# Raw expert blocks under the first tile's staging buffer, gathered rows under the others'

## The chip, the cores and the metric

The kernel runs on 1 core of one Trainium2 chip. The metric is the device time of one execution in microseconds (us), as the median of several runs. The core has a matrix engine (PE, with its weight loads as PEld), a vector engine (DVE), a scalar engine (ACT), a general one (POOL) and a queue engine that only issues transfers (SP). Sixteen DMA engines move what SP and POOL issue.

## What is computed

One decoder layer on 512 tokens of 1024 channels. The change lies in its second half, where every token picks, for each of 8 heads, the 16 best of 16,384 experts, each a pair of rows u and v:

```python
def peer_ffn(h, w_query, sub_keys, expert_u, expert_v):
    ...
    e = (jnp.take_along_axis(i1, flat // PEER_TOPK, axis=-1) * PEER_NKEYS
         + jnp.take_along_axis(i2, flat % PEER_TOPK, axis=-1))
    g = jax.nn.softmax(sc, axis=-1).astype(h.dtype)
    def one_chunk(args):
        xc, ec, gc = args
        u = expert_u[ec]
        a = jax.nn.gelu(jnp.einsum('cd,chkd->chk', xc, u))
        return jnp.einsum('chk,chkd->cd', gc * a, expert_v[ec])
```

## The kernel before, in words

The kernel splits the tokens of this part. Some 320 of them (two tiles of 128 and half of a third, `DS`) are computed densely: all 128 blocks of 128 experts are loaded in full, and a token's gate for an expert that it didn't pick is zero. The other 192 (192 = the fourth tile and half of the third, moved beside it) are computed by gathering the rows that they picked.

The dense part needs a table of gates, [expert, block, token]. It is built before the blocks ("the gate stage"): for each token DVE, POOL and ACT write one-hot rows, PE multiplies them (L853), and ACT copies the result out of PSUM into a staging buffer (`stage`, L1106), 4 tokens a group, 80 groups (`w_staged` counts them): 32 into `staged[0]`, 32 into `staged[1]`, 16 into `staged[2]`. SP stores each staging buffer to DRAM, to `w_scratch`: tile 0 and tile 1 whole (8 MB each, pieces of 512 B), tile 2 in slices of blocks, `SLICES` (pieces of 256 B, 32 KB a block). Later each block reads its own row of it back (`load_gates`, into `w_row`).

Memory is reused by address, in KB of a partition: `staged[0]` lies at 35.5 to 99.5, `staged[1]` at 99.5 to 163.5, `staged[2]` at 67.5 to 99.5, over the upper half of `staged[0]`. In the kernel before the raw blocks (`u_raw` and `v_raw`, 99.5 to 131.5) lie under `staged[1]`, and the gathered rows (`u_rows`, `v_rows`, 35.5 to 83.5) under `staged[0]` and `staged[2]`. The row of gates (`w_row`), and the parts of a block split in two for precision (`u_hi`, `u_lo`, `v_hi`, `v_lo`), lie under `staged[1]` in both.

Block b of the dense part, in the order in which each engine runs it (all run in order, and semaphores join them): ACT copies `u_raw` to `u_hi` (`u_high`, L1167), DVE makes `u_lo` (`u_low`, L1555), PE multiplies 24 times (`first`, L887 to L889), ACT takes the gelu (L1182), DVE multiplies with the gates (`gated`, L1568), ACT and DVE split that in two (`g_both`, L1188 and L1572), and PE multiplies with `v_hi` and `v_lo` 16 times (`second`, L900 to L910). On PE the order is first(b+1), second(b). On DVE, `block_step(b)` is gated(b), u_low(b+2), g_lo(b); then comes `own(n, q)`, a quarter of the gathered tokens' work (b = 4n + q): q = 0 and 1 use three gathered u rows each (L1587), q = 2 and 3 three v rows each (L1615); then `next_values`, which is v_low(b+1). On ACT, `block_step(b)` is gelu(b), u_high(b+2), g_hi(b), v_high(b+1).

The raw buffers hold 4 blocks (`STEP`). SP refills a place when its block has been used (`refill(n, q)`): u, v and gate row of block b+4. POOL gathers 6 u rows and 6 v rows of 512 KB for each 4 blocks (`gather_u`, `gather_v`, then `next_rows`).

SP's order in the handover, before: store tile 0, store tile 1, store slice 0 of tile 2; wait for tile 1's store; load blocks 0 to 3; wait for slice 0; load four gate rows; store slice 1; refill(0, 0); store slice 2; refill(0, 1) to refill(0, 3); wait for slices 1 and 2; the loop. POOL, behind its last one-hot rows, waits for `w_stored[0]`, gathers u rows, waits for slices 0 and 1, gathers v rows.

Of the kernel before, what the change touches and what calls it, by code (L numbers as in the profile page):

```python
# [13 lines left out]
P = 128  # L14
D = 1024
S = 512
NT = S // P
KD = D // P
# [6 lines left out]
PH, NK, QD = 8, 128, 128  # L25
# [22 lines left out]
ROWS = GRP + XGRP  # L48
DT = NT - 1
EX = P // 2  # L50
DS = DT * P - EX
STEP = 4
# [6 lines left out]
EARLY = 32  # L59
OWN, SPLIT = NT - 1, NT - 2  # L60
POOL_ROWS = 2
SLICES = [(0, 8), (8, 64), (64, NK)]


def bucket_onehot():
# [81 lines left out]
def build(nc, x, c, ada_w, ada_b, rows_g, w_in, ln_gb, w_s, b_s, rel, w_branch, w_out, w_query, keys,  # L147
# [3 lines left out]
    with ctx:  # L151
# [3 lines left out]
        def sem(name):  # L155
            return ctx.enter_context(nc.semaphore(name))
# [5 lines left out]
        def at(name, kb, shape, dt=F32):  # L162
            t = nc.alloc_sbuf_tensor_at(name, shape, dt, offset=base_byte + int(kb * 1024))
            return t[tuple(slice(None) for _ in shape)]
# [86 lines left out]
        staged = [at("staged0", 35.5, [P, NK, P]), at("staged1", 99.5, [P, NK, P]), at("staged2", 67.5, [P, NK, EX])]  # L251


        u_raw = at("u_raw", 99.5, [P, STEP, KD, P])
        v_raw = at("v_raw", 115.5, [P, STEP, D])
        w_row = at("w_row", 131.5, [P, STEP, DS])
        u_hi = at("u_hi", 137.5, [P, 2, KD, P], F32R)
        u_lo = at("u_lo", 145.5, [P, 2, KD, P], F32R)
# [2 lines left out]
        gel = at("gel", 169.5, [P, 2, DS])  # L261
        gated = at("gated", 172.5, [P, 2, DS])
        g_both = at("g_both", 177, [P, 2, DS, 2], F32R)
        u_rows = at("u_rows", 35.5, [P, ROWS, D])
        v_rows = at("v_rows", 59.5, [P, ROWS, D])
        acc_x = at("acc_x", 24, [P, D])
        fold = at("fold", 83.5, [P, 2, EX])
        y_out = at("y_out", 99.5, [P, DT, D])
        y_parts = at("y_parts", 111.5, [P, D])
        junk3 = at("junk3", 115.5, [P, D])  # L270
# [90 lines left out]
        w_stored = [sem(f"w_stored{i}") for i in range(2)]  # L361
        w_slice = [sem(f"w_slice{i}") for i in range(len(SLICES))]
        u_raw_in, v_raw_in, w_row_in = ([sem(f"{n}{q}") for q in range(STEP)]
# [20 lines left out]
        def turn(j, q):  # L384

            return j // STEP + 1
# [39 lines left out]
        def _(sp):  # L426
# [56 lines left out]
            def load_experts(q, b):  # L483

                sp.dma_start(u_raw[:, q].rearrange("p k e -> p (k e)"), u_blocks[b]).then_inc(u_raw_in[q], 16)
                sp.dma_start(v_raw[:, q], v_blocks[b]).then_inc(v_raw_in[q], 16)

            def load_gates(q, b):
                sp.dma_start(w_row[:, q], w_rows[b]).then_inc(w_row_in[q], 16)

            def store_gates(t, lo, hi, signal):

                sp.wait_ge(w_staged, min(DS_GROUPS * (t + 1), ALL_GROUPS))
                n = min(P, DS - t * P)
                sp.dma_start(w_dram[:, lo:hi, t * P:t * P + n], staged[t][:, lo:hi, 0:n]).then_inc(signal, 16)
# [6 lines left out]
            for half in range(2):  # L502
                rows, cut = slice(half * EX, (half + 1) * EX), slice(half * EX, (half + 1) * EX)
                sp.dma_start(ex_picks[rows, 0], starts[EX:P, cut]).then_inc(ex_in, 16)
                sp.dma_start(ex_picks[rows, 1], picks[SPLIT][EX:P, 2, cut]).then_inc(ex_in, 16)
            store_gates(0, 0, NK, w_stored[0])
            store_gates(1, 0, NK, w_stored[1])
            store_gates(2, *SLICES[0], w_slice[0])
            sp.wait_ge(w_stored[1], 16)
            for q in range(STEP):  # L510
                load_experts(q, q)
            sp.wait_ge(w_stored[0], 16)
            sp.wait_ge(w_slice[0], 16)
            for q in range(STEP):
                load_gates(q, q)

            def refill(n, q):
                b = n * STEP + q
                sp.wait_ge(u_lo_done, b + 1)
                sp.wait_ge(v_lo_done, b + 1)  # L520
                sp.wait_ge(gated_done, b + 1)
                load_experts(q, b + STEP)
                load_gates(q, b + STEP)

            for q in range(STEP):
                if q + 1 < len(SLICES):
                    store_gates(2, *SLICES[q + 1], w_slice[q + 1])
                refill(0, q)
            for q in range(1, len(SLICES)):
                sp.wait_ge(w_slice[q], 16)  # L530
# [13 lines left out]
        def _(pool):  # L544
# [96 lines left out]
            multiplied(pool, *group("h2T"))  # L641
            pool.wait_ge(idx_ready, 1)

            pool.wait_ge(w_stored[0], 16)
            for part in range(2):
                gather_u(0, part)
            pool.wait_ge(w_slice[0], 16)
# [28 lines left out]
        def _(pe):  # L676
# [45 lines left out]
            def project(*jobs):  # L722
                for _, b, j in jobs:
                    w = arrived("in", b)
                    cut = slice(j * P, (j + 1) * P)
                    product(("in", b, j), [(w[:, k, cut], hT[:, k, :]) if b < 2 else (hT[:, k, cut], w[:, k, :])
                                           for k in range(KD)])
# [213 lines left out]
        def _(act):  # L941
# [42 lines left out]
            def gates(jobs):  # L984

                for _, b, j in jobs:
                    o = take(act, "in", b, j)
                    gate, f = (ga, b - 5) if b < 7 else (gg, b - 7)
                    act.activation(gate[:, j, f * HALF:(f + 1) * HALF], o[:, :], ACT.Tanh, scale=0.5)\
                        .then_inc(free("in", b, j), 1)  # L990
# [171 lines left out]
            def u_high(j, q):  # L1162
                r = q % 2
                act.wait_ge(u_raw_in[q], 16 * turn(j, q))
                if not isinstance(j, int) or j >= 2:
                    act.wait_ge(a_full, j - 1)
                act.activation(u_hi[:, r], u_raw[:, q], ACT.Copy).then_inc(u_hi_done, 1)  # L1167
# [24 lines left out]
            def own_gelu(n):  # L1192

                act.wait_ge(u_rows_used[1], n + 1)
                act.activation(dots_gelu, dots, ACT.Gelu_apprx_tanh).then_inc(own_gelu_done, 1)

            u_high(0, 0)
            u_high(1, 1)
            v_high(0, 0)
# [32 lines left out]
        def _(dve):  # L1232
# [342 lines left out]
            def next_values(b, q):  # L1575
                if not isinstance(b, int) or b + 1 < NK:
                    v_low(b + 1, (q + 1) % STEP)
# [47 lines left out]
            for q in range(STEP):  # L1625
                block_step(q, q)
                own(0, q)
                next_values(q, q)
            dve.wait_ge(w_slice[len(SLICES) - 1], 16)
            two = ident.rearrange("p (t a) -> p t a", a=2)  # L1630
# [58 lines left out]
```

## Time and profile before

| | us |
|---|---|
| median of 3 runs | 1782.34 (1781.99 to 1784.86) |
| the profiled execution's own time | 1783.35 |
| its span in the profile | 1781.6 |
| PE busy | 1600.2 (90%) |
| DVE busy | 1306.5 (73%) |
| POOL busy | 828.0 (46%) |
| ACT busy | 600.4 (34%) |

The span is cut by the profile into 40 slices of 44.5 us. A digit in them is a share in tenths. The gate stage ends at 791 us, in the eighteenth slice; the 128 blocks fill the rest. All stretches below are in us from the start of the span.

### The profile page before, as it was taken

To read this page: it belongs to the slowest core of one execution; us is meant where nothing else is said; L and a number is where in the kernel's file an instruction comes from. 1 tells how busy PE (TensorE), PEld (TensorE's weight loads), DVE (VectorE), ACT (ScalarE), POOL (GpSimd) and SP (SyncE) were. 2 spreads that over 40 slices of the span, in tenths; PEclk is the share of its full clock that TensorE was granted. 3 is DMA by queue.
4 is the path that set the end of the run, shared out by engine and by line. 5 is a ranking of instruction groups with operands and counts; after the bars stand their busy time and mean duration, and the time that the engine had idled before them with its cause. 6 is when DMAs were issued, how large, how long until landed. Compare 5 with 4: busy or idle time off the path is not lost.

```text
span 1781.6 us, 24636 instructions
## 1 busy us (share of the span) xinstructions
PE 1600.2 (90%) x7621; PEld 1241.8 (70%) x7621; DVE 1306.5 (73%) x2599; ACT 600.4 (34%) x1043; POOL 828.0 (46%) x800
## 2 busy tenths in 40 slices
PE   6899999999797764666699999999999999999997
PEld 2444454444475653556599999999999999999996
DVE  0534231213259999974699999999999999999998
ACT  1120022320213665332233433343343344334333
POOL 1000100000103996672566666666666666666662
PEclk9899999999898985898799999999999999999998
DMA  9946211111300000679999999999999999999993
GB/s 360 341 154 224 94 60 47 48 47 66 126 1 1 1 1 13 190 208 337 370 388 388 378 387 380 385 388 385 383 384 384 381 385 385 386 384 384 384 383 120
DMA packets 192870, 450.39 MB, mean 253 GB/s; under 512 B 30323, under 2 KB 79731, under 8 KB 192444
## 3 DMA queue, kind: packets, MB, share of 16 engines
q1 hardware_dynamic: 136636, 245.21, 38.7%
q0 software_dynamic: 56192, 204.66, 29.3%
q8 instruction: 21, 0.34, 0.1%
q14 instruction: 21, 0.17, 0.0%
HBM read 426.13 MB, written 23.10 MB: 252 GB/s over the span
## 4 chain that ended last, share of the span: by engine, by line
PE 78%; DVE 11%; DMA 6%; POOL 2%; issue 1%; ACT 1%; SPq 1%; POOLq 0%; DVEq 0%; ACTq 0%
PE bank L693 22%; PE bank L888 8%; PE bank L889 8%; PE bank L887 8%; PE bank L910 7%; PE bank L908 6%; PE bank L909 6%; PE bank L900 3%; PE bank L901 3%; DMA w_scratch<-staged 2%; PE bank L814 2%; DMA u_raw<-u_by_key 2%; DMA ada_blk<-ada_w 2%; POOL hot L625 1%; PE bank L778 1%
## 5 line engine op out<-in xcount | busy, mean ns | idle before, releaser
L887 PE MATMUL bank<-h_hi,u_hi 128*128 128x320 f32 x1024 | 316.6, 309 | 22.9 <-DVE u_lo L1555 22.9
L888 PE MATMUL bank<-h_lo,u_hi 128*128 128x320 f32 x1024 | 317.4, 310 | 0.0
L889 PE MATMUL bank<-h_hi,u_lo 128*128 128x320 f32 x1024 | 317.3, 310 | 0.0
L601 POOL DMA_INDIRECT v_rows<-v_exp,small x192 | 263.1, 1370 | 91.5 <-POOL small L597 51.8
L601 POOL DMA_INDIRECT u_rows<-u_exp,small x192 | 240.9, 1255 | 92.5 <-POOL small L597 52.0
L1174 ACT ACTIVATE v_hi<-v_raw 128x1024 fp32r<-128x1024 f32 x128 | 135.8, 1061 | 245.6 <-PE bank L910 245.6
L1555 DVE TENSOR_TENSOR u_lo<-u_raw,u_hi 128x1024 fp32r<-128x1024 f32 x128 | 157.6, 1231 | 75.3 <-ACT u_hi L1167 75.3
L887 PEld LDWEIGHTS bank<-h_hi,u_hi 128*128 128x128 f32 x1024 | 193.1, 189 | 28.3 <-issue 23.1
L910 PE MATMUL bank<-v_hi,g_both 128*128 128x512 f32 x512 | 204.4, 399 | 0.0
L909 PE MATMUL bank<-v_lo,g_both 128*128 128x512 f32 x512 | 203.2, 397 | 0.0
L908 PE MATMUL bank<-v_hi,g_both 128*128 128x512 f32 x512 | 203.2, 397 | 0.0
L693 PE MATMUL bank<-ring,hT 128*128 128x512 f32 x448 | 197.8, 598 | 0.8 <-ACT zv L1004 0.8
L888 PEld LDWEIGHTS bank<-h_lo,u_hi 128*128 128x128 f32 x1024 | 193.0, 188 | 6.8
L889 PEld LDWEIGHTS bank<-h_hi,u_lo 128*128 128x128 f32 x1024 | 193.0, 188 | 0.0
L597 POOL COPY small<-idx_by 128x3 uint32 (+1 forms) x128 | 119.2, 931 | 148.0 <-DVE acc L1615 81.4
L1615 DVE SCALAR_TENSOR_TENSOR acc<-v_rows,small,acc 128x1024 f32<-128x1024 f32 x128 | 164.1, 1282 | 8.6 <-DMA v_rows<-v_exp,small 6.4
L693 PEld LDWEIGHTS bank<-ring,hT 128*128 128x128 f32 x448 | 84.7, 191 | 109.1 <-issue 109.1
L1561 DVE TENSOR_TENSOR v_lo<-v_raw,v_hi 128x1024 fp32r<-128x1024 f32 x128 | 155.9, 1218 | 0.0
L1587 DVE SCALAR_TENSOR_TENSOR u_rows<-u_rows,h_own 128x1024 f32<-128x1024 f32 x128 | 153.5, 1218 | 0.0
L1167 ACT ACTIVATE u_hi<-u_raw 128x1024 fp32r<-128x1024 f32 x128 | 134.7, 1052 | 44.7 <-DMA u_raw<-u_by_key 44.7
L1182 ACT ACTIVATE gel<-bank 128x320 f32<-128x320 f32 x128 | 56.0, 438 | 242.4 <-PE bank L889 242.4
L900 PE MATMUL bank<-v_hi,g_both 128*128 128x512 f32 x256 | 101.9, 398 | 19.0 <-DVE g_both L1572 19.0
(216 smaller groups left out, 2589.7 us busy)
## 6 DMA issues: line engine op xcount, KB each, us to landing
u_raw<-u_by_key SPq DMA_DIRECT2D x128, 512.0 KB, 6.1
v_raw<-v_exp SPq DMA_DIRECT2D x128, 512.0 KB, 8.1
w_row<-w_scratch SPq DMA_DIRECT2D x128, 160.0 KB, 9.3
ada_blk<-ada_w SPq DMA_DIRECT2D x9, 2048.0 KB, 17.7
ring<-w_in SPq DMA_DIRECT2D x9, 2048.0 KB, 8.4
w_scratch<-staged SPq DMA_DIRECT2D x2, 8192.0 KB, 34.6
ring<-ada_w SPq DMA_DIRECT2D x3, 2048.0 KB, 13.0
xr<-x SPq DMA_DIRECT2D x8, 512.0 KB, 11.7
```

What stands on the lines that cost most here:

```text
L601: pool.indirect_dma_start(out=rows[:, s], out_offset=None, in_=table, in_offset=bass.IndirectOffsetOnAxis(ap=ix[:, s:s + 1], axis=0))\
L693: last = pe.matmul(o[:, :], a, b, start=(k == 0), stop=(k == len(pairs) - 1))
L887: pe.matmul(o, u_hi[:, r, k], h2_hi[:, k], start=(k == 0), stop=False)
L888: pe.matmul(o, u_hi[:, r, k], h2_lo[:, k], start=False, stop=False)
L889: last = pe.matmul(o, u_lo[:, r, k], h2_hi[:, k], start=False, stop=(k == KD - 1))
L900: pe.matmul(o, both, v_hi[:, r, half], start=is_first, stop=False)
L908: pe.matmul(o, hi, v_hi[:, r, half], start=is_first, stop=False)
L909: pe.matmul(o, hi, v_lo[:, r, half], start=False, stop=False)
L910: last = pe.matmul(o, lo, v_hi[:, r, half], start=False, stop=is_last)
L1555: dve.tensor_tensor(u_lo[:, r], u_raw[:, q], u_hi[:, r].bitcast(F32), ALU.subtract)\
L1561: dve.tensor_tensor(v_lo[:, r], v_raw[:, q], v_hi[:, r].bitcast(F32), ALU.subtract)\
L1615: ins = dve.scalar_tensor_tensor(into, v_rows[:, s], coef[:, s:s + 1], into, ALU.mult, ALU.add)
```

## The change

The raw blocks move under `staged[0]`, to the lower half that `staged[2]` doesn't cover. The gathered u rows move under `staged[1]`, the v rows and `fold` under `staged[2]`. Tile 2 is stored in two slices instead of three: blocks 0 to 7, and 8 to 127. SP waits for tile 0's store as soon as it has issued it, loads blocks 0 to 3, and only then comes to tile 1's store. The whole second slice is issued behind the four gate rows and ahead of all refills. POOL's first u gather waits for tile 1's store instead of tile 0's, and ACT waits for tile 1's store before it writes `u_hi`. POOL's first v gather still waits for slices 0 and 1, but slice 1 is now all that is left of the tile.

```diff
-SLICES = [(0, 8), (8, 64), (64, NK)]
+SLICES = [(0, 8), (8, NK)]
...
-        u_raw = at("u_raw", 99.5, [P, STEP, KD, P])
-        v_raw = at("v_raw", 115.5, [P, STEP, D])
+        u_raw = at("u_raw", 35.5, [P, STEP, KD, P])
+        v_raw = at("v_raw", 51.5, [P, STEP, D])
...
-        u_rows = at("u_rows", 35.5, [P, ROWS, D])
-        v_rows = at("v_rows", 59.5, [P, ROWS, D])
+        u_rows = at("u_rows", 99.5, [P, ROWS, D])
+        v_rows = at("v_rows", 67.5, [P, ROWS, D])
...
-        fold = at("fold", 83.5, [P, 2, EX])
+        fold = at("fold", 91.5, [P, 2, EX])
...
             store_gates(0, 0, NK, w_stored[0])
+            sp.wait_ge(w_stored[0], 16)
+            for q in range(STEP):
+                load_experts(q, q)
             store_gates(1, 0, NK, w_stored[1])
             store_gates(2, *SLICES[0], w_slice[0])
             sp.wait_ge(w_stored[1], 16)
-            for q in range(STEP):
-                load_experts(q, q)
-            sp.wait_ge(w_stored[0], 16)
             sp.wait_ge(w_slice[0], 16)
             for q in range(STEP):
                 load_gates(q, q)
+            store_gates(2, *SLICES[1], w_slice[1])
...
             for q in range(STEP):
-                if q + 1 < len(SLICES):
-                    store_gates(2, *SLICES[q + 1], w_slice[q + 1])
                 refill(0, q)
...
-            pool.wait_ge(w_stored[0], 16)
+            pool.wait_ge(w_stored[1], 16)
             for part in range(2):
                 gather_u(0, part)
...
+            act.wait_ge(w_stored[1], 16)
             u_high(0, 0)
```

## Rows read from the trace of the kernel before

**Rows 1.** The span in 40 equal slices: PE's busy tenths.
```profile
PE   6899999999797764666699999999999999999997
```
**Rows 2.** Stretches: length, each engine's busy us (instructions), granted clock, DMA share, GB/s.
```profile
720.00:750.60 30.60, 22.81 (x150) 20.31 (x151) 30.30 (x91) 10.75 (x18) 22.41 (x30) 0.83 0.97 275
750.60:769.70 19.10, 15.94 (x112) 13.33 (x112) 19.10 (x56) 8.37 (x14) 15.86 (x22) 1.00 0.00 0
769.70:791.80 22.10, 17.96 (x126) 14.97 (x125) 19.81 (x58) 9.56 (x16) 17.95 (x24) 1.00 0.96 274
791.80:808.20 16.40, 0.00 (x0) 0.00 (x0) 0.00 (x0) 0.00 (x0) 5.09 (x7) 0.60 1.04 345
...
830.00:839.00 9.00, 9.00 (x54) 8.36 (x54) 7.76 (x13) 3.93 (x7) 6.72 (x6) 1.00 1.08 295
839.00:861.00 22.00, 7.70 (x44) 6.79 (x42) 5.21 (x5) 0.44 (x1) 11.99 (x15) 0.74 1.06 403
...
900.00:1000.00 100.00, 100.00 (x555) 91.30 (x555) 93.75 (x124) 40.47 (x60) 68.57 (x56) 1.00 1.01 384
```
**Rows 3.** The chain that ended last, 769 to 862: start, length, what.
```profile
769.68 38.51 DMA w_scratch<-staged
...
812.31 10.13 DMA w_row<-w_scratch
...
829.86 31.71 DMA u_raw<-u_by_key
```
**Rows 4.** SP's instructions in order of time: start, length of the issue.
```profile
814.56 0.42 SPq L495 DMA_DIRECT2D w_scratch<-staged  x1
...
829.86 20.52 SPq L485 DMA_DIRECT2D u_raw<-u_by_key  x1
```
**Rows 5.** DMA issues at 720, 814, 829, and all u gathers: size, us to landing.
```profile
w_scratch<-staged SPq DMA_DIRECT2D x1, 8192.0 KB, 30.7
...
w_scratch<-staged SPq DMA_DIRECT2D x1, 1792.0 KB, 15.3
...
w_scratch<-staged SPq DMA_DIRECT2D x1, 2048.0 KB, 29.7
...
u_rows<-u_exp,small POOLq DMA_INDIRECT x192, 8.1
```
**Rows 6.** PE's instructions in order of time, with the idle time before them.
```profile
813.95 0.61 PE L887 MATMUL bank<-h_hi,u_hi 128*128 128x320 f32 x1 [22.90 <-DVE u_lo L1555]
...
824.71 0.47 PE L900 MATMUL bank<-v_hi,g_both 128*128 128x512 f32 x1 [1.28 <-DVE g_both L1572]
...
864.46 0.76 PE L900 MATMUL bank<-v_hi,g_both 128*128 128x512 f32 x1 [17.77 <-DVE g_both L1572]
...
874.34 0.39 PE L900 MATMUL bank<-v_hi,g_both 128*128 128x512 f32 x1
...
881.59 0.39 PE L900 MATMUL bank<-v_hi,g_both 128*128 128x512 f32 x1
```
**Rows 7.** ACT, POOL and DVE in order of time, each with its idle time before.
```profile
811.49 1.06 ACT L1167 ACTIVATE u_hi<-u_raw 128x1024 fp32r<-128x1024 f32 x1 [19.72 <-DMA u_raw<-u_by_key]
...
789.71 0.18 POOL L597 COPY small<-idx_by 128x3 uint32<-128x3 uint32 x1
...
793.52 0.94 POOL L601 DMA_INDIRECT u_rows<-u_exp,small  x1 [0.30 <-issue]
...
830.04 0.69 POOL L597 COPY small<-idx_by 128x3 uint32<-128x3 uint32 x1 [31.11 <-DMA w_scratch<-staged]
...
844.14 1.28 DVE L1615 SCALAR_TENSOR_TENSOR acc<-v_rows,small,acc 128x1024 f32<-128x1024 f32 x1 [6.37 <-DMA v_rows<-v_exp,small]
...
848.87 0.49 DVE L1568 TENSOR_TENSOR gated<-gel,w_row 128x320 f32<-128x320 f32 x1
```
**Rows 8.** Stretches with PE idle, and its restart: columns as in rows 2.
```profile
849.00:851.00 2.00, 0.00 (x0) 0.00 (x0) 0.35 (x1) 0.00 (x0) 1.70 (x2) 0.64 1.04 407
...
864.00:867.00 3.00, 2.54 (x6) 2.09 (x7) 2.96 (x4) 1.35 (x2) 0.00 (x0) 0.50 1.04 403
```

## The prediction

> **What bounds the kernel now.** I read the slices first [rows 1]. PE is at 9 tenths in every slice from the twenty-first on (from 888 us): once the blocks run, PE sets the pace, and this stretch can't get shorter by moving transfers. The hundred microseconds from 900 to 1000 [rows 2] say the same: PE busy 100.00 of 100, at full clock, with DMA at 384 GB/s. The `second` of block 4 starts on PE at 874.34 and that of block 5 at 881.59 [rows 6]: a block costs 7.25 us. Everything behind 874.34 I take as fixed, since the code there is the same. So the question is when the second(4) starts in the changed kernel. I call that time S4; before it is 874.34.
>
> Next the stretch in front of it, by windows [rows 2]. In the gate stage, to 791, PE is held by hot rows; DMA moves 275 GB/s to 750.6 (tile 0's store), nothing at all to 769.7, then 274 GB/s (tile 1's store). From 791.8 to 808.2 every compute engine but POOL stands still. The chain [rows 3] names it: tile 1's store, from 769.68 for 38.51 us; behind it a gate row that takes 10.13 us; and then a u block from 829.86 for 31.71 us. PE has two holes [rows 6]: 22.90 us before 813.95 and 17.77 us before 864.46, the second(3). A handover in which PE never waited after its second(0) at 824.71 would have S4 at 824.71 + 4 x 7.25 = 853.7; it is 20.6 later. These two holes are what the change can touch.
>
> **Tile 1's store.** Before, POOL gathers six u rows (3.15 MB) beside it: it takes their indices at 789.71 and issues the third at 793.52 [rows 7]; from 791.8 to 808.2 DMA is fully busy, at 345 GB/s [rows 2]. The change holds these gathers back until the store has landed. Tile 0's store, of the same size and with nothing beside it, took 30.7 us [rows 5]. So tile 1's should land at 769.7 + 30.7 = 800.4 instead of 808.2 (769.68 + 38.51): 7.8 us earlier. I call this T1.
>
> **The first loads.** SP gets an added wait, for tile 0's store, at about 750.7. Queued behind it are eight loads and tile 1's store, which isn't ready before 769.7. The eight issues took from 808.2 to 812.3 [rows 3], 4.1 us, and the 4.19 MB take 10.4 us at 403 GB/s [rows 2]: done by about 765, in a window in which DMA is empty. The gate stage shouldn't notice: PE does 112 instructions in 19.1 us with DMA idle (5.9 a microsecond) and 126 in 21.3 us of work with DMA full (5.9) [rows 2]. Cost zero; without that cover (if the loads ran past 769.7) they would delay T1 by what is left. ACT then starts `u_hi` right at T1. Before it waited until 811.49 [rows 7], 3.3 us behind the store, and PE began 2.46 us after ACT [rows 6, 7]. So first(0) starts at about 800.5 + 2.5 = 803.0 instead of 813.95.
>
> **The gate rows and second(0).** Slice 0 (256 KB) follows tile 1's store in the queue, 1 us by 274 GB/s, so the gate rows are issued at 801.4 with no loads in front of them; before, the first took 10.13 us [rows 3] behind 4 MB. The second(0) then hangs on PE alone, two `first`s behind 803.0: about 812.5 instead of 824.71. That is 12.2 us gained at this point, before the next steps.
>
> **POOL's first u gather.** Moved from 789.7 to T1. Queued behind its wait on POOL are only the v gathers. By the old pace the third row is issued 3.8 us after the wake [rows 7] and takes 8.1 [rows 5]: 812.5, just when own(0, 0) wants it. If it is some microseconds late this doesn't count, because DVE has to wait for v rows further on, at 840, and would reach that point at about 827.
>
> **The merged slice.** This is what sets the end. The first v gather needs all of tile 2 stored. Before, slice 1 landed at 829.86 (814.56 + 15.3 [rows 4, 5]); now it is blocks 8 to 127, 120 x 32 KB = 3.93 MB, issued at 801.4 + 2.25 (four gate issues, 812.31 to 814.56 [rows 3, 4]) = 803.7. I call its landing T2. Between T1 + 1 = 801.4 and T2 the DMA engines have to move the gate rows (0.66 MB), the u gathers (3.15 MB) and this slice, 7.74 MB. Refills queue behind the slice. The rate has two bounds: 403 GB/s, where 256 B pieces, gathers and loads mix (839 to 861), gives 19.2 us, T2 = 821, and with a late start 822; 295 GB/s (830 to 839) [rows 2] gives 26.2, T2 = 827.6. A third way: old slice 1 could only move once the gate rows in front of it were in (822.44), so its 1.835 MB took 7.4 us, 247 GB/s; 3.93 MB at that rate is 15.9 us, and the other 3.81 MB at 403 is 9.5: T2 = 826.8. I take 826, nearest to the last two.
>
> A rule of the Trainium skill ("DMA: Bandwidth & Descriptors", Bandwidth) says that for transfers between HBM and SBUF the HBM side binds, at about 358 GB/s a core. By it the 7.74 MB would take 21.6 us and T2 would be 823. The 403 GB/s of 839 to 861 [rows 2] speak against such a limit here, so it stands outside the sum.
>
> **From T2 to S4.** Before, w_slice 1 landed at 829.86, POOL went on at 830.04, and DVE had its v rows at 844.14 [rows 7]: 14.3 us. Nothing in this piece of POOL's code changes. It has other company now (three refills, 3.6 MB, in place of slice 2 with its 29.7 us [rows 5]); as a bound from below I take 12 (third issue 3.8 after the wake, as with the u rows, and 8.1 to land), from above 18. From there DVE does three v rows and v_low(3), and starts gated(3) at 848.87 [rows 7], 4.7 later. Then come gated(3), u_low(5) and g_lo(3), 2.2 us together: 0.4 for the first [rows 7], and 1.8 for the others, since from the landing of the load at 861.57 to second(3) at 864.46 [rows 3, 6] there were 2.9, of which ACT's `u_hi` took 1.06. Before, u_low(5) waited for `u_raw` of block 5, stuck behind slice 2: issued at 829.86, blocked for 20.52 us in SP's queue [rows 4], landed at 861.57 [rows 3]. In the changed kernel block 4's and 5's loads stand directly behind the merged slice. Slice 2, issued half a microsecond ahead of the old block 5, landed 29.7 us on [rows 5], at 859.0, and block 5 followed it by 2.6, so block 4 lands at T2 + 2.6 = 828.6 and block 5, 1.2 MB later, well before 840. Block 4's lateness holds second(2) until about 831.5 instead of 827, which is hidden: DVE waits for v rows until 840.3 anyway. So the second hole stays, but shorter: second(3) at T2 + 14.3 + 4.7 + 2.2 = 847.2, against 864.46. PE has by then been idle from about 838, 9 us. Before, the clock was at 0.64 in 849 to 851, that is 3 to 5 us into the hole, and 0.50 (1.2 GHz) in the first microseconds of work after it [rows 8]; so I expect the low level again, and with it the same 9.88 us from second(3) to second(4) [rows 6]. S4 = 847.2 + 9.9 = 857.1.
>
> **The sum.** 874.3 - 857.1 = 17.2 us earlier, and all behind moves with it. The profiled execution took 1783.35 us, so its like would take 1766.1; the median of the runs is 1.0 lower: 1765.1. The slots of `fold`, of the output buffers and of the split blocks change addresses or nothing: no term.
>
> **DMA after S4.** It must also keep up. All four next refills and the second u gathers (9.9 MB from T2 on) take 25 us at 403 GB/s, until 851; the second u rows are wanted by DVE at about 854. That is close, but DMA has no more work than before: its 4.19 MB of first loads have left the handover. Cost taken as zero, 3 us at worst.
>
> **Rivals.**
> (a) *The merged slice crawls, and the kernel is slower.* Slice 2 took 29.7 us for 2.1 MB beside gathers [rows 5], 71 GB/s. If the merged slice gets only that share of the engines for its whole length, it lands at 803.7 + 55.7 = 859, S4 is 859 + 31.1 = 890, and the time 1798. It decides at T2 = 843: later than that and the kernel is slower. For it: one single gate on 3.93 MB now holds POOL, where before it was on half. Against it: beside slice 2 some 9 MB of others moved (9 us at 295 and 22 at 403 GB/s [rows 2], less its own 2.1 MB), beside the merged slice 3.8, and then it has the engines to itself. The Trainium skill (same page, Queues, rings and completion order) says that each DMA engine goes round-robin between queues at packet granularity; by that a 256 B store beside 4 KB gathers gets little until the gathers end, and it names this rival's mechanism. Chance 8%.
> (b) *Tile 1's store isn't sped up.* The gathers may have used what the store leaves free: 38.5 us again, T1 = 808.2. Everything moves by 7.8: S4 = 865, the time 1773. Against it: 274 GB/s alone and 0.96 busy [rows 2]. Chance 12%.
> (c) *The second hole nearly closes.* T2 at 822, v rows 12 behind it, and PE idle so shortly that its clock stays up (7.25 instead of 9.9): S4 = 822 + 12 + 6.9 + 7.25 = 848.2, the time 1756.2. Chance 13%.
> (d) *The change doesn't do what it says:* the loads are early, but the head is bound by something not in the rows (SP blocked, POOL late), and only the 3.3 us between store and `u_hi` are won: 1779. Chance 5%.
> (e) *It ends where it was:* the later v gate eats the head's gain, T2 = 843. Chance 3%.
>
> **How the numbers follow.** My forecast, 1765, has the other 59%; its own bounds (T2 822 to 828, v rows 13 to 18 us behind, 3 us for the refills) give 1760 to 1773. With (b) inside and (c) at the lower end the range is 1755 to 1774; outside remain (a), (d), (e) and half of (c). Some 0.2% (3.6 us) is what a measurement of this kernel can tell from no change. Faster by more than that: forecast, (b) and (c), and some of (d), 0.86. Within: (d)'s rest and (e), 0.05. Slower: (a) and a little for what no row shows, 0.09.
>
> **What would show it.** Tile 1's store landing in 30.7 us (step 1); `u_hi` starting within 0.5 us of it (step 2); second(0) at 812 to 813; the merged slice landing at 822 to 828; DVE waiting for v rows until T2 + 13 to 18; PE's second hole at 7 to 12 us with the clock low behind it; block 5's load no longer the last one in. Wrong it would be if the merged slice lands behind 843, if the blocks behind S4 take more than 7.25 us, or if the gate stage ends later than 791.

## The result and the profile after

The changed kernel takes 1769.22 us (median of 4 runs, 1767.11 to 1770.59) against 1782.16 for the kernel before (4 runs): a ratio of 0.9927, with a 95% interval of 0.9914 to 0.9941, or 12.9 us less. Measured again on another occasion the ratio was 0.9939 (0.9922 to 0.9957). I had said 1765, between 1755 and 1774. The direction and the path held; the gain was 12.9 instead of 17.2.

The profiled execution of the changed kernel took 1767.11 us, with a span of 1765.3. That is 16 us less than the profiled one of before, and part of it is no doing of the change: this execution reached the handover 3.6 us sooner (SP issued tile 1's store at 766.13, before at 769.68 [rows 3]), out of stages that are the same in both. So I measure everything from that issue. By the same token it is chance that this execution came so near to the 1766.1 that the sum gave for it.

The chain that ended last, from 787 to 849 (start, length, what):

```profile
787.57 0.61 ACT staged L1105
788.20 9.80 DMA w_scratch<-staged
...
800.20 26.71 DMA w_scratch<-staged
...
830.54 11.19 DMA v_rows<-v_exp,small
841.84 1.28 DVE acc L1615
...
845.51 1.14 DVE v_lo L1561
...
848.73 0.77 PE bank L899
```

Beside [rows 3]: the gate row's 10.13 us and the u block's 31.71 us are gone. In their place stands one long store, the merged slice, and the v rows behind it. SP's queue in order of time (start, length of the issue) shows how the first pieces moved:

```profile
747.07 0.34 SPq L485 DMA_DIRECT2D u_raw<-u_by_key  x1
...
766.13 27.83 SPq L495 DMA_DIRECT2D w_scratch<-staged  x2
798.08 2.06 SPq L489 DMA_DIRECT2D w_row<-w_scratch  x4
800.20 0.42 SPq L495 DMA_DIRECT2D w_scratch<-staged  x1
806.88 18.45 SPq L485 DMA_DIRECT2D u_raw<-u_by_key  x1
```

The two holes of PE, which were 22.90 and 17.77 us [rows 6], are now three (PE in order of time; the brackets hold the idle time before and what ended it):

```profile
799.34 0.61 PE L886 MATMUL bank<-h_hi,u_hi 128*128 128x320 f32 x1 [11.89 <-DVE u_lo L1555]
...
831.22 0.76 PE L899 MATMUL bank<-v_hi,g_both 128*128 128x512 f32 x1 [7.16 <-DVE g_both L1572]
...
848.73 0.77 PE L899 MATMUL bank<-v_hi,g_both 128*128 128x512 f32 x1 [7.86 <-DVE g_both L1572]
...
858.03 0.39 PE L899 MATMUL bank<-v_hi,g_both 128*128 128x512 f32 x1
```

The second(4) starts at 858.03. From the issue of tile 1's store that is 91.9 us, against 104.7 before (874.34 - 769.68): 12.8 less, the whole of the gain. (In the second profiles of both, further down, it is shorter by 10.7, and the medians of the second measurement are 10.5 apart.) Behind it 907.27 us remain in both kernels (1765.3 - 858.03 and 1781.6 - 874.34), so the blocks indeed run as before.

The stretches (length, busy us of PE, PEld, DVE, ACT and POOL with their instructions, clock, DMA share, GB/s), to be held against [rows 2]:

```profile
750.60:769.70 19.10, 15.91 (x112) 13.29 (x111) 19.10 (x57) 8.16 (x15) 16.02 (x21) 1.00 0.56 212
...
796.60:800.20 3.60, 0.86 (x3) 0.90 (x4) 2.24 (x2) 3.31 (x4) 2.24 (x2) 0.50 0.56 141
...
820.00:826.00 6.00, 4.06 (x27) 3.71 (x25) 1.41 (x2) 0.44 (x2) 0.00 (x0) 1.00 0.85 192
...
900.00:1000.00 100.00, 100.00 (x551) 91.09 (x550) 94.13 (x119) 39.38 (x59) 66.44 (x55) 1.00 1.01 390
```

DMA moves 212 GB/s in the window in which it moved nothing, and PE does 112 instructions there as before. Part of the 212 is tile 1's store, which here began at 766.13: the loads were issued from 747.07 on, and from 762 to 766 DMA is idle again. And there are two stretches in which DMA does badly: just behind tile 1's store it stands half idle (0.56), and from 820, with the slice nearly alone in the queues, it moves 192 GB/s.

That second stretch has a border. The u rows are in by about 813.5, and from then to 824 every packet is one of the slice's. Yet they don't move at one rate (the same columns):

```profile
816.00:820.00 4.00, 3.96 (x19) 3.16 (x18) 4.00 (x9) 0.47 (x2) 0.00 (x0) 1.00 1.27 290
```

From 821 to 824 the same slice, alone, moves at 218 GB/s and a share of 0.95. In the kernel before, old slice 1 is alone in the same way from 824 to 828, at 290 GB/s and 1.27. So pieces of 256 B move at 290 GB/s for some microseconds and then fall to 218, and old slice 1, of 1.8 MB, was through before it fell. What decides between the two levels no run here shows.

### The profile page after: what moved, and what is told of

It reads as the page before. It is cut to its first block, busy times and chain, and to the rows that moved or that the text cites. A ratio compares the mean times of both kernels' runs of the same rounds, so it can differ in the third digit from the quotient of the medians.

```text
span 1765.3 us, 24635 instructions
## 1 busy us (share of the span) xinstructions
PE 1600.4 (91%) x7621; PEld 1244.3 (70%) x7621; DVE 1306.7 (74%) x2599; ACT 600.3 (34%) x1043; POOL 822.2 (47%) x800
## 4 chain that ended last, share of the span: by engine, by line
PE 78%; DVE 11%; DMA 4%; POOL 3%; issue 2%; ACT 1%; SPq 1%; POOLq 0%; DVEq 0%; ACTq 0%
PE bank L692 22%; PE bank L888 8%; PE bank L887 8%; PE bank L886 8%; PE bank L909 7%; PE bank L907 7%; PE bank L908 7%; PE bank L899 3%; PE bank L900 3%; DMA w_scratch<-staged 2%; POOL hot L624 2%; PE bank L813 2%; DMA ada_blk<-ada_w 2%; PE bank L777 1%; PE bank L733 1%
## 5 line engine op out<-in xcount | busy, mean ns | idle before, releaser
L600 POOL DMA_INDIRECT u_rows<-u_exp,small x192 | 236.9, 1234 | 93.2 <-POOL small L596 52.1
L1615 DVE SCALAR_TENSOR_TENSOR acc<-v_rows,small,acc 128x1024 f32<-128x1024 f32 x128 | 164.1, 1282 | 12.9 <-DMA v_rows<-v_exp,small 10.7
## 6 DMA issues: line engine op xcount, KB each, us to landing
w_scratch<-staged SPq DMA_DIRECT2D x2, 8192.0 KB, 30.7
ring<-ada_w SPq DMA_DIRECT2D x3, 2048.0 KB, 12.9
```

Of the source, the lines that this page charges most:

```text
L600: pool.indirect_dma_start(out=rows[:, s], out_offset=None, in_=table, in_offset=bass.IndirectOffsetOnAxis(ap=ix[:, s:s + 1], axis=0))\
L1615: ins = dve.scalar_tensor_tensor(into, v_rows[:, s], coef[:, s:s + 1], into, ALU.mult, ALU.add)
```

## The experiments

To have one number for a kernel that the wobble of the earlier stages can't reach, I took from each profile the time from the issue of tile 1's store to the end of the span ("tail"). It is 1011.9 us in the kernel before, 999.2 in the changed one. Second profiles of four kernels, at the end of this section, show how far it can be trusted: they differ from the first by 0.0 to 3.9 us.

Two theories stood against each other. A: the handover is bound by the bytes that the DMA engines have to move between tile 1's store and the second(4), each kind at its own rate; the gain is the 4.19 MB of first loads that went into an idle window. B: the gain is that tile 1's store lands earlier because nothing moves beside it, and the loads are a detail.

**The held gather alone.** The kernel before, with one line:

```diff
-            pool.wait_ge(w_stored[0], 16)
+            pool.wait_ge(w_stored[1], 16)
             for part in range(2):
                 gather_u(0, part)
```

> The kernel before, with one line of the change: POOL's first u gather waits for tile 1's store. Theory A (the handover is bound by the bytes that the DMA engines have to move in it): holding the gathers back only moves their 3.15 MB from beside the store to behind it. The store lands in 30.7 us instead of 38.5, but the 7.8 us are given back before the second(4); the time stays within 3 us of the kernel before, 1779 to 1785. Rival B (the earlier landing of the store is itself the gain, and the early loads are a detail): the head moves by 7.8 us and most of it stays, 1774 to 1776.

Measured: 1782.88 us (12 runs), ratio 1.0007 (0.9990 to 1.0024). The store does land in 30.7 us, and nothing is left of it at the end. The chain shows where it went:

```profile
770.13 30.69 DMA w_scratch<-staged
...
805.06 17.95 DMA w_row<-w_scratch
...
830.53 25.78 DMA u_raw<-u_by_key
```

The gate row that took 10.13 us before now takes 17.95, with loads and gathers under way together. The time is in A's range, and B's, 1774 to 1776, is outside the interval: B falls.

**The loads put back.** The changed kernel, with the first loads where they were:

```diff
-            sp.wait_ge(w_stored[0], 16)
-            for q in range(STEP):
-                load_experts(q, q)
             store_gates(1, 0, NK, w_stored[1])
             store_gates(2, *SLICES[0], w_slice[0])
             sp.wait_ge(w_stored[1], 16)
+            for q in range(STEP):
+                load_experts(q, q)
+            sp.wait_ge(w_stored[0], 16)
             sp.wait_ge(w_slice[0], 16)
```

> The changed kernel, with the first eight expert loads put back behind tile 1's store; layout, merged slice and POOL's wait stay changed. Theory A: 4.19 MB come back into the handover, which at 403 GB/s is 10.4 us; the gain of 12.9 falls to about 2.5, time 1777 to 1783. Rival B: only the 3.3 us between the store and u_hi come back, time 1771 to 1774.

Measured: 1777.10 us (12 runs), ratio 0.9981 (0.9964 to 0.9997); tail 1007.3 (1774.6 less the store's start at 767.3). The tail says 8.1 us for the loads' place, the medians 6.5 to 7.9. That is in A's range and out of B's, but below the 10.4 that the bytes at 403 GB/s would make. Against the kernel before, 2 to 5 us of gain are left without it, in the merged slice, its place or the layout; I didn't take these apart.

**More to store.** The changed kernel with blocks 8 to 63 of tile 2 stored once more, to a buffer that nothing reads:

```diff
+            sp.dma_start(w_extra_dram[:, 8:64], staged[2][:, 8:64, 0:EX]).then_inc(w_extra, 16)
             store_gates(2, *SLICES[1], w_slice[1])
...
             pool.wait_ge(w_slice[1], 16)
+            pool.wait_ge(w_extra, 16)
```

> The changed kernel with 1.84 MB more to store: blocks 8 to 63 of tile 2 are also stored to a second DRAM buffer that nothing reads, ahead of the large slice, and POOL and DVE wait for it too. If the slice's landing is on the path at the rate that it had (7.74 MB in 26.7 us, 290 GB/s): 6.3 us later, 1774 to 1777. If it is hidden behind something else: 1769 to 1771.

Measured: 1779.06 us (12 runs), ratio 0.9988 (0.9971 to 1.0004), above my 1774 to 1777; tail 1006.8, 7.6 more than the changed kernel. The issues (size, us to landing):

```profile
w_scratch<-staged SPq DMA_DIRECT2D x1, 3840.0 KB, 34.8
w_extra_scratch<-staged SPq DMA_DIRECT2D x1, 1792.0 KB, 17.8
```

The large slice lands 34.8 us behind its issue instead of 26.7: 8.1 us for 1.835 MB, or 227 GB/s. Nearly all of it comes out at the end. So the slice's landing is on the path, and its pieces are slower than I had taken them. (The median, 8.5 to 9.8 above the changed kernel's, is somewhat more than the tail says.)

**The slice alone.** The changed kernel with the first u gathers behind the slice:

```diff
             pool.wait_ge(w_stored[1], 16)
-            for part in range(2):
-                gather_u(0, part)
             pool.wait_ge(w_slice[0], 16)
             pool.wait_ge(w_slice[1], 16)
+            for part in range(2):
+                gather_u(0, part)
```

> The changed kernel, with POOL's first u gathers held until tile 2 is stored whole: the large slice then has the DMA engines nearly to itself, so its landing is a measurement of the term that the prediction mis-sized. If its 256 B pieces move at the 247 GB/s that I took from slice 1: 15.9 us and the gate rows in front, 17 to 18 us from issue to landing. If they are slower alone, 20 to 24 us. All gathers then come behind it, DVE waits for u rows; second(4) some 5 us later than in the changed kernel, time 1772 to 1777.

Measured: 1772.74 us, ratio 0.9955 (0.9935 to 0.9974); tail 1000.5. The slice's issue, and a stretch in which little else moves:

```profile
w_scratch<-staged SPq DMA_DIRECT2D x1, 3840.0 KB, 19.9
```
```profile
806.00:820.00 14.00, 14.00 (x76) 13.36 (x75) 2.97 (x4) 4.09 (x6) 0.00 (x0) 0.87 0.99 226
```

The rate is 226 GB/s with DMA at a share of 0.99, and 19.9 us to land, just under my second case of 20 to 24 and clearly over the first. It is a mean over the higher level and the lower one: from 806 to 808 it is 268 GB/s, from 808 to 822 it is 219. The tail is only 1.3 us longer than the changed kernel's, where I had said 5: another exchange of one transfer's place for another's that comes out near zero, as A has it.

**The v rows by part.** The changed kernel with two large slices, each of which frees its part of the v rows' memory:

```diff
-SLICES = [(0, 8), (8, NK)]
+SLICES = [(0, 8), (8, 48), (48, NK)]
...
             store_gates(2, *SLICES[1], w_slice[1])
+            store_gates(2, *SLICES[2], w_slice[2])
...
             pool.wait_ge(w_slice[1], 16)
-            for part in range(2):
-                gather_v(0, part)
+            gather_v(0, 0)
+            pool.wait_ge(w_slice[2], 16)
+            gather_v(0, 1)
```

> The changed kernel, with the large slice cut in two (blocks 8 to 47, and 48 to 127), both issued one behind the other where the one stood; POOL gathers the first three v rows when the first of them is stored, the other three when all is. If the merged slice's landing sets the end through POOL's v gather (theory A and the prediction alike): first v rows some 10 us earlier, second(3) no longer held by them but by block 4's load, which still follows the whole slice; second(3) about 8 us earlier, the second v part then just in time: 1759 to 1763. If instead the DMA engines' total work alone sets it (strong form of A): the same bytes in the same time, 1767 to 1770.

Measured: 1765.80 us (6 runs), ratio 0.9915 (0.9886 to 0.9943); tail 994.4, 4.8 less. DVE no longer waits for v rows in front of second(3), and PE has no hole there. Its last long hole lies in front of second(2), and block 4's load ends it, as I had said, but later than I had reckoned (waits: engine, line, for what, us in total, times, longest):

```profile
ACT u_hi L1168 <- DMA u_raw<-u_by_key: 12.5, 2, 12.2
```
```profile
838.99 0.76 PE L901 MATMUL bank<-v_hi,g_both 128*128 128x512 f32 x1 [11.47 <-DVE g_both L1574]
```

The gathers that now run beside the second slice hold up its landing (31.0 us behind its issue) and with it the load in its queue. The result lies between both expectations. The medians are 3.4 and 4.8 us below the changed kernel's two, but the intervals of the ratios overlap, and the tail is that of one profile: that the order of the same bytes is worth something here speaks against A's strong form without settling it. The reason stays open. That gathers fill the stretch in which the changed kernel has slow pieces alone would be one, but from 820 to 826 DMA moves 219 GB/s here against 192 there, and that is worth well under a microsecond.

**The order of SP's queue.** As the last one, with block 4's loads between the slices:

```diff
-SLICES = [(0, 8), (8, NK)]
+SLICES = [(0, 8), (8, 48), (48, 96), (96, NK)]
...
             for q in range(STEP):
                 refill(0, q)
+                if q + 2 < len(SLICES):
+                    store_gates(2, *SLICES[q + 2], w_slice[q + 2])
```

> As x3_v_by_part, but tile 2 behind block 7 in three slices (blocks 8 to 47, 48 to 95, 96 to 127), with block 4's loads and gate row between the first two and block 5's between the last two. x3 still waited 11.5 us on PE for block 4's u load, which stood behind the whole tile. If the order of the SP queue matters: that wait goes, second(4) comes 84 to 87 us behind the issue of tile 1's store (91.9 in the changed kernel, 87.0 in x3), time 1761 to 1765. If only the sum of the bytes matters, as theory A says in its strong form: 87 to 92 us, time 1765 to 1769.

Measured: 1766.80 us (6 runs), ratio 0.9921 (0.9899 to 0.9943); tail 995.4. The time lies in the second range. The second(4) came 85.3 us behind the issue, in the first range, but out of a hole of 6.05 us, and the next block then took 10.0 us instead of 7.25. Block 4's load is in time now, and the wait reappears at DVE, for v rows of both parts:

```profile
833.97 1.28 DVE L1618 SCALAR_TENSOR_TENSOR acc<-v_rows,small,acc 128x1024 f32<-128x1024 f32 x1 [5.69 <-DMA v_rows<-v_exp,small]
849.14 1.28 DVE L1618 SCALAR_TENSOR_TENSOR acc_x<-v_rows,small,acc_x 128x1024 f32<-128x1024 f32 x1 [8.42 <-DMA v_rows<-v_exp,small]
```

The same bytes in another order than in the last kernel, and a tail within a microsecond of its tail. Between these two the order decides who waits, not for how long all wait.

**Larger pieces.** If the piece size makes the slice slow, tile 2's gates belong in a buffer of their own, in which a partition's blocks are contiguous on both sides. Each block then fetches its gate row in two loads:

```diff
+        w_dram2 = nc.dram_tensor("w_scratch2", [P, NK, EX], F32, kind="Internal").ap()
...
-                sp.dma_start(w_row[:, q], w_rows[b]).then_inc(w_row_in[q], 16)
+                sp.dma_start(w_row[:, q, 0:2 * P], w_rows[b]).then_inc(w_row_in[q], 16)
+                sp.dma_start(w_row[:, q, 2 * P:DS], w_rows2[b]).then_inc(w_row_in[q], 16)
...
+                to = w_dram2[:, lo:hi] if t == 2 else w_dram[:, lo:hi, t * P:t * P + n]
+                sp.dma_start(to, staged[t][:, lo:hi, 0:n]).then_inc(signal, 16)
```

> The changed kernel, with tile 2's gates stored to a DRAM buffer of their own, [expert, block, 64 tokens], where a partition's 120 blocks are one contiguous run instead of 120 pieces of 256 B; in return every block's gate row comes back in two loads (256 and 64 tokens). If the large slice is slow for its small pieces: it lands in 19 to 21 us instead of 26.7, and second(4) comes about 6 us earlier. The price is 128 more pieces of 256 B for every block in the long run; if DMA has room there, the time is 1762 to 1765; if it has none, up to 128 x 0.3 us later.

Measured: 1762.35 us (6 runs), ratio 0.9889 (0.9870 to 0.9908), and again 1761.29, ratio 0.9887 (0.9870 to 0.9905); tail 990.4 in both profiles, 8.8 less than the changed kernel. The issue, and the same stretch as above:

```profile
w_scratch<-staged SPq DMA_DIRECT2D x1, 3840.0 KB, 14.9
```
```profile
806.00:820.00 14.00, 14.00 (x76) 13.34 (x75) 3.05 (x5) 4.09 (x6) 4.84 (x6) 0.86 1.01 397
```

14.9 us instead of 26.7, beside gathers in both, and 397 GB/s, loads and gathers included; I had said 19 to 21, for I had left the whole stretch at a lower rate. The second load for each block costs nothing that can be seen: from second(4) at 853.82 to the end of the span are 907.3 us, as ever. (The 0.3 us a block in my price came from no run.) This version beats both kernels, by 20 us and by 8.

The path has changed, too. DVE finds its v rows in time, and now waits for the first u rows, which POOL may gather only when tile 1 is stored and which move beside the slice (waits of DVE in the kernel with larger pieces; in the changed kernel the same wait is 1.0 us):

```profile
DVE u_rows L1591 <- DMA u_rows<-u_exp,small: 10.4, 1, 10.4
```

It gets them at 823.83, 53.1 us behind the issue of tile 1's store, in the changed kernel at 809.84, 43.7 us behind. Second(1) hangs on it, and from there on PE doesn't wait any more. So by this trace the slice itself is off the path, and the next limit is tile 1's store with the u rows behind it.

**Half a tile early.** The idle window isn't full: the first loads take 10 of its 19 us. So, on top of the last one, tile 1's store in two halves of its tokens, the first as soon as it is staged:

```diff
-            store_gates(1, 0, NK, w_stored[1])
+            for half in range(2):
+                cut = slice(half * EX, (half + 1) * EX)
+                sp.wait_ge(w_staged, DS_GROUPS + (half + 1) * DS_GROUPS // 2)
+                sp.dma_start(w_dram[:, :, P + half * EX:P + (half + 1) * EX], staged[1][:, :, cut]).then_inc(w_stored[1], 16)
```

> As x7_tile2_apart, but tile 1's store is cut in two by tokens: tokens 0 to 63 go when they are staged (48 groups), so that they move in what is left idle between the first expert loads and the end of tile 1, some 8 us; the rest goes at 64 groups. The price: all of tile 1 moves in 256 B pieces, 8.39 MB at 226 instead of 274 GB/s, 6.5 us of DMA time. Theory A: 8 us of bytes leave the handover and 6.5 come in, less what of the first half is done by 770; a gain of 1.5 to 5 us on x7, 1757 to 1761. Rival (the store is not the bound once the gate stage ends 9 us before it lands, because the gathers need POOL's pace): no change against x7, 1761 to 1763.

Measured: 1762.49 us, ratio 0.9885 (0.9865 to 0.9905), beside 0.9887 without it. No gain. The stretch, and the two stores in the order of their issue (size, us to landing):

```profile
770.00:792.00 22.00, 18.36 (x128) 15.37 (x129) 21.63 (x64) 9.44 (x17) 18.42 (x24) 1.00 0.98 222
```
```profile
w_scratch<-staged SPq DMA_DIRECT2D x1, 4096.0 KB, 26.6
w_scratch<-staged SPq DMA_DIRECT2D x1, 4096.0 KB, 31.0
```

The window is used, but in pieces of 256 B the tile moves at 222 GB/s, where whole it moved at 274: 7 us more DMA time for 8.39 MB, which is what the window gave (without this edit DMA is at a share of 0.18 in the 8.7 us from 762.0 to 770.7). So tile 1 lands 31.0 us behind the moment when it is all staged, against 30.7 whole; the u rows follow as in the last kernel, and the tail is 991.7 against 990.4. The time is what the rival expected, but the rival wasn't put to the test, since the store didn't land earlier.

**How steady the handover is.** Four kernels have a second profile.

> The kernel before, once more, for a second profile: from the issue of tile 1's store to the end of the span 1011.9 us in the first one. If the handover runs the same way each time (as the changed kernel's did: 999.2 and 999.0), 1011 to 1013; if not, anywhere from 1006 to 1013.

The kernel before had a tail of 1009.7 this time (1779.3 - 769.6), 2.2 less than in the first profile: block 5's load was blocked 16.47 us in the queue instead of 20.52. The changed kernel's was 999.0, after 999.2.

> The changed kernel itself, on the chip of these runs: 0.9914 to 0.9941 of the kernel before.

> The kernel before with POOL's first u gather held back, once more, for a second profile. Over 12 runs its median was that of the kernel before (1782.9 against 1781.3), but the runs fell in two groups (five at 1777.7 to 1778.9, seven at 1782.9 to 1785.3), and the profiled one lay in the lower: from the issue of tile 1's store to the end of the span 1006.3 us, 5.6 less than in the kernel before. If the groups are two courses of the handover, a profile of the upper one shows that stretch at 1010 to 1013. If they come from the stages ahead of the handover, as the 3.6 us by which the first profile of the changed kernel began it earlier do, the stretch is 1006 to 1007 again, whatever the time.

The held gather alone had 1010.1 (1774.3 - 764.2), after 1006.2: the handover itself isn't quite steady, yet the longer tail belonged to the shorter time (1776.08 us), since that execution reached the handover 5.9 us sooner. So both of my explanations of the two groups hold in part, and with two profiles I can't say which makes the groups. What stands is the median of 12.

> The changed kernel with tile 2's gates in a DRAM buffer of their own, on the chip of the next kernel: 0.987 to 0.991 of the kernel before.

## Why the prediction was right, and where its size was off

Step by step, in us from the issue of tile 1's store, the profile of the changed kernel beside what I wrote:

| | predicted | measured |
|---|---|---|
| tile 1's store lands | 30.7 | 30.7 |
| the merged slice is issued | 34.0 | 34.1 |
| from there until it lands | 22.3 | 26.7 |
| from the landing until DVE has its v rows | 14.3 | 14.9 |
| from there to second(3) | 6.9 | 6.9 |
| second(3) to second(4) | 9.9 | 9.3 |
| second(4): the sum of the five rows above | 87.4 | 91.9 |

- **Tile 1's store, first loads, head:** right. `u_hi` started at 796.88, in the same microsecond as the landing; the second(0) followed at 809.14, 43.0 us behind the store's issue where I had 42.8. But the 7.8 us of the store aren't a gain of their own, and by itself the wait that brings them is worth nothing (1.0007). The sum had them right only because it charged the gathers to the next term.
- **The merged slice is the mis-sized term:** 4.4 of the 4.5 us. From T1 + 1 on I had 7.74 MB in 24.6 us, 315 GB/s; measured are 29.1 us at 274 GB/s (797.8 to 826.9). I see three parts, by estimates that no run separates. I took 247 GB/s for 256 B pieces from old slice 1. That was a short transfer, in which they moved at 290; in a long one they fall to 218, and the mean of the slice alone is 226. 3.93 MB then take 17.4 us instead of 15.9. And I counted DMA as busy from T1 + 1 on, while it was at a share of 0.46 in the next 2.4 us (126 GB/s): SP waits for slice 0 before the gate rows, POOL copies indices, and little is queued meanwhile. That is about 1.3 us. I had also rounded T2 down from 826.8 to 826. These make 3.6. What else the trace shows is the slice's last 2.9 us, at a share of 0.64 and 161 GB/s.
- **The sign "the merged slice landing at 822 to 828" failed**, though the trace says 826.9: from the issue of tile 1's store it is 60.8 us, and counted from the 769.7 of the prediction that is 830.5.
- **From T2 on:** right within a microsecond in each step. Block 4's load did hold second(2) (to 831.22) and was hidden as I said, since DVE then waited 10.7 us for v rows.
- **Clock:** the hole in front of second(3) was 7.9 us and the one before it 7.2, and behind both PE restarted slowly: 0.76 us for the first instruction of `second` instead of 0.39. The granted clock was 0.50 from 849 to 851, as forecast. From second(3) to second(4) took 9.3 us where the blocks take 7.25.
- **DMA keeps up behind second(4):** right, no cost. The Trainium skill's figure of about 358 GB/s a core ("DMA: Bandwidth & Descriptors", Bandwidth), which the page gives for a core whose neighbour streams too, was no limit here: DMA moved 397 GB/s over 14 us with the larger pieces. By an estimate from it the slice would have landed at 823, sooner than I had said and further from what came.
- **Rivals:** (a), the slice that crawls, didn't come: 26.7 us instead of 55.7; the gathers beside it are in by about 813.5. It had the sign of my error right, since the slice was slower than my figure. (b) was refuted by the 30.7 us. (c) needs an earlier landing; larger pieces gave it (50.3 us behind the issue of tile 1's store, where (c) had 52.3) and closed the second hole, and its time of 1756 was still out of reach (1761 to 1762), because the u rows were then late. (d) and (e) didn't come.
- **Slips that moved nothing:** the hole before the old second(3) began at 846.7, so 849 to 851 is 2.3 to 4.3 us into it, not 3 to 5. And the 9.9 MB behind T2 are three refills and both sets of gathers, not what the sentence names; with the fourth refill they are 11.1 MB, 27.6 us at 403 GB/s.

What I had not seen as the common cause is theory A: the two chains in my sum (the head, and the slice with its v rows) share one resource, and the gain is mainly the loads that left it. A sum over the bytes alone would have said 10.4 and a little more; putting the loads back cost 6.5 to 8.1.

## What to carry to other kernels

Where a handover is bound by DMA, first add up its bytes, each at the rate of its own piece size, and look for windows in which DMA stands idle: a transfer moved into one is a gain, while one that only changes places with another in the full stretch was worth little here (nothing for the u gathers held back, at most 5 us for the v rows by part), however much earlier the first link of the chain lands. Take the rate of a small-piece transfer from one that runs alone and is as long as the one you forecast: a short one moved at 290 GB/s here, the rest of a long one at 218. After each gain read again which wait ends last; with larger pieces it was another one. And when such a store is on the path, give it a buffer in which its pieces are contiguous before you cut or reorder it.

## What the runs showed of the hardware that I hadn't expected

- A long store in pieces of 256 B moves at 222 to 227 GB/s on the whole (three measurements), in pieces of 512 B at 274, and the same 3840 KB as contiguous runs a partition, beside gathers, within a stretch at 397. DMA's busy share is 0.96 to 1.01 in these stretches, so the share doesn't tell slow pieces from fast ones; GB/s does.
- Within such a store the pieces of 256 B have two levels: 290 GB/s at a busy share of 1.27 (the changed kernel from 813.5 to 819, the kernel before from 824 to 828), then 218 at 0.95 (821 to 824). The cause is open.
- Reading a gate row back in two loads, of 1024 and 256 B a partition, instead of one of 1280 B, costs nothing measurable even though DMA runs at 397 GB/s and a share of 1.03 in the blocks.
- The gate stage itself doesn't take the same time in each execution: from tile 0's store to tile 1's 49.7 to 49.9 us in all the other profiles and 53.4 in the one of the doubled slice, whose code is the same there.
